# Two-block transformer on one core: the compressed keys' norm ahead on VectorE, the low-rank keys' scale two units later, and two unread products on TensorE

## The reference

```python
# half A: 8 query heads over 2 key heads, head width 64, three branches
kc = apply_rope(rmsnorm(compress(k_cmp), kc_gain))     # 15 compressed keys per key head: 30 rows of 64
p_c = masked_softmax(q @ kc, cmp_end <= t)             # branch 1: compressed
# branches 2 and 3: selected blocks and a window, which for 256 positions are all causal keys
out_a = g0 * (p_c @ vc) + g1 * (p_s @ v_slc) + g2 * (p_w @ v_win)
# half B: 8 low-rank heads, width 96 (64 without and 32 with a rotation)
q, k = rmsnorm(q, q_gain), rmsnorm(k, k_gain)
q, k = rope of the last 32 columns of each
out_b = softmax(q @ k * 96 ** -0.5, causal) @ v
mixed = concat(rmsnorm(out_a), rmsnorm(out_b)) @ w_out
h = x + mixed
return h + peer_ffn(rmsnorm(h))                        # 16 experts for each of 8 heads and position, gathered from HBM
```

## Time and profile before

| | before |
|---|---|
| median of 3 runs | 1548.1 us (1545.95 to 1549.3) |
| the profiled execution's own time | 1549.46 us |
| its span, first to last instruction | 1547.7 us |
| PE busy | 1345.1 us, 87% |
| DVE busy | 966.0 us, 62% |
| ACT busy | 554.8 us, 36% |
| POOL busy | 361.1 us, 23% |
| mean granted clock of PE | 0.935 of full |
| DMA | 407.37 MB, 263 GB/s over the span |

### The profile page before, as it was taken

How to read it: one execution, slowest core, us unless ns; L and a number is a source line. 1 busy time by engine, 2 the same in 40 slices (tenths; PEclk the granted TensorE clock), 3 DMA queues, 4 the chain that set the end, 5 groups by cost and what they waited for, 6 DMA issues and landing times.

```text
span 1547.7 us, 19406 instructions
## 1 busy us (share of the span) xinstructions
PE 1345.1 (87%) x6346; PEld 951.5 (61%) x6346; DVE 966.0 (62%) x2292; ACT 554.8 (36%) x1147; POOL 361.1 (23%) x364
## 2 busy tenths in 40 slices
PE   6997899997997999979798587989798878888877
PEld 4896789986986998968487443434343434343333
DVE  3485655555456555565786667677767777677753
ACT  3453544444554444453573222222212222222221
POOL 0102000000001000010510444444444444345440
PEclk9997999998998999989899899989999999899988
DMA  9524456554313755544401599999999999999995
GB/s 345 216 82 90 143 190 190 190 185 168 109 55 113 230 187 190 163 152 146 170 1 55 199 420 421 420 421 421 421 422 421 422 421 421 422 421 422 421 420 224
DMA packets 97323, 407.37 MB, mean 263 GB/s; under 512 B 6875, under 2 KB 44444, under 8 KB 60412
## 3 DMA queue, kind: packets, MB, share of 16 engines
q0 software_dynamic: 39632, 277.12, 43.8%
q1 hardware_dynamic: 57644, 129.66, 24.6%
HBM read 405.42 MB, written 1.07 MB: 263 GB/s over the span
## 4 chain that ended last, share of the span: by engine, by line
PE 48%; DMA 24%; issue 12%; DVE 11%; ACT 3%; POOL 2%; DVEq 0%; SPq 0%; POOLq 0%; ACTq 0%
DMA arena_v<-in_peer_uv,prob 17%; PE ps L579 12%; PE ps L580 12%; PE ps L581 12%; PE ps L685 6%; DMA uv_mk<-in_peer_uv,prob 3%; DMA arena_u<-in_peer_uv,prob 2%; DVE w_low L1478 1%; PE ps L517 1%; POOL small L1322 1%; PE ps L659 1%; DMA ring<-in_v_a 1%; PE ps L526 1%; PE ps L510 1%; DVE arena_u L2045 1%
## 5 line engine op out<-in xcount | busy, mean ns | idle before, releaser
L1478 DVE TENSOR_TENSOR w_low<-ring,w_high 128x1024 fp32r<-128x1024 f32 (+1 forms) x168 | 195.3, 1205 | 202.3 <-ACT w_high L966 202.0
L966 ACT ACTIVATE w_high<-ring 128x1024 fp32r<-128x1024 f32 (+1 forms) x168 | 166.1, 1038 | 243.2 <-PE ps L581 243.2
L685 PE MATMUL ps<-arena_u,sco 128*128 128x512 f32 x256 | 132.3, 642 | 55.7 <-ACT sco L1138 55.7
L579 PE MATMUL ps<-hT_high,w_high 128*128 128x256 f32 x512 | 145.1, 283 | 0.3
L580 PE MATMUL ps<-hT_low,w_high 128*128 128x256 f32 x512 | 144.7, 283 | 0.0
L581 PE MATMUL ps<-hT_high,w_low 128*128 128x256 f32 x512 | 144.7, 283 | 0.0
L1138 ACT ACTIVATE sco<-const,prob 128x128 f32<-128x128 f32 x256 | 83.9, 391 | 165.0 <-DVE prob L2055 154.1
L1149 ACT ACTIVATE prob<-prob 128x4 f32<-128x4 f32 (+1 forms) x65 | 13.4, 206 | 346.6 <-DVE prob L2045 346.6
L1328 POOL TENSOR_SCALAR small<-small 128x1 f32<-128x1 f32 x8 | 4.2, 529 | 531.6 <-ACT arena_v L996 531.6
L685 PE MATMUL ps<-arena_v,sco 128*128 128x512 f32 x256 | 125.1, 613 | 0.0
L685 PEld LDWEIGHTS ps<-arena_u,sco 128*128 128x128 f32 x256 | 49.1, 200 | 117.6 <-ACT sco L1138 71.8
(11 more groups left out here) (362 smaller groups left out, 2960.1 us busy)
## 6 DMA issues: line engine op xcount, KB each, us to landing
ring<-in_w_up SPq DMA_DIRECT2D x32, 1024.0 KB, 5.6
ring<-in_w_down SPq DMA_DIRECT2D x32, 1024.0 KB, 4.8
qkring<-in_qk_a SPq DMA_DIRECT2D x8, 1024.0 KB, 5.6
qkring<-in_qk_b SPq DMA_DIRECT2D x8, 1024.0 KB, 4.7
ring<-in_peer_wq SPq DMA_DIRECT2D x8, 1024.0 KB, 9.0
ring<-in_w_in SPq DMA_DIRECT2D x8, 860.0 KB, 4.5
ring<-in_v_a SPq DMA_DIRECT2D x4, 1024.0 KB, 12.8
ring<-in_w_out_a SPq DMA_DIRECT2D x4, 1024.0 KB, 9.4
```

What stands on the lines that cost most here:

```text
L579: pe.matmul(dst, a[0], b[0], start=start, stop=False, skip_group_check=True)
L685: last = pe.matmul(ps[2 * t + n][:, :], diag[:, k % N_DIAG, :], slots[k][:, D + n * HALF:D + (n + 1) * HALF], start=False, stop=(final and ...
L966: sc.activation(w_split[pair][0][:, part], ring[:, slot, part], ACT.Copy)\
L1478: ve.tensor_tensor(w_split[pair][1][:, part], ring[:, slot, part], w_split[pair][0][:, part].bitcast(F32), ALU.subtract)\
```

## The change

Five edits, all inside `hybrid_attention`.

1. On DVE the two calls for `mk` leave their place ahead of the compressed keys: `low_rank_mean(1)` now stands behind `kc_ready`, and `low_rank_weigh(mk, gain_mk)` where `low_rank_scale(1, mk)` stood.
2. `low_rank_scale(1, mk)` moves into step 3 of the loop over units, between `share_of(1, 1)` and `add_bias`.
3. PE turns the low-rank pairs in another order, `LOW_RANK_TURNS` (side 0 is queries, side 1 keys): two query pairs first, then two key pairs. The second wait for `mqk_ready` stands at `n` = 2, which is step 5, instead of `n` = 1.
4. ACT's `take_low_rank` follows the same table.
5. PE issues `N_IDLE` = 2 products of 128x512 into `ps[7]`, behind the transposes of `nat` and ahead of the wait for `kc_ready`. Nobody reads them: `ps[7]` is overwritten by the transposed compressed probabilities.

```diff
--- before.py
+++ after.py
@@ -54,6 +54,7 @@
     [0, 512, 128, 128, 128, 128, 128, 128, 24, 256, 128, 32]).tolist()
 N_CMP = 15
 MLA_HEADS = 8
+LOW_RANK_TURNS = ((0, 0), (0, 1), (1, 0), (1, 1), (0, 2), (1, 2), (0, 3), (1, 3))
 QK = 96
 
 P_HEADS = 8
@@ -62,6 +63,7 @@
 N_UNITS = P_HEADS * NT
 CHOOSE_STEPS = 47
 GROUP = 4
+N_IDLE = 2
 N_DIAG = 4
 PEER_SLOT = 2
 
@@ -847,6 +849,8 @@
                     if c % 2:
                         last.then_inc(sem("turned_a"), 1)
 
+                for _ in range(N_IDLE):
+                    pe.matmul(ps[7][:, :], ident, nat[:, 0, 0:HALF], start=True, stop=True)
                 pe.wait_ge(sem("kc_ready"), count.take("kc_ready"))
                 pe.transpose(ps[5][:, P:P + 30], kc_twice, ident[0:30, 0:30]).then_inc(sem("kc_turned"), 1)
                 pe.wait_ge(sem("hT_a"), count.take("hT_a", 4))
@@ -873,12 +877,13 @@
 
                 def turn_low_rank(n, bank):
 
-                    if n < 2:
+                    if n in (0, 2):
                         pe.wait_ge(sem("mqk_ready"), count.take("mqk_ready"))
+                    side, pair = LOW_RANK_TURNS[n]
                     for head in range(2):
                         for t in range(NT):
                             last = pe.transpose(ps[bank][0:QK, head * S + t * P:head * S + t * P + P],
-                                                (mq, mk)[n % 2][:, t, 2 * (n // 2) + head, :], ident)
+                                                (mq, mk)[side][:, t, 2 * pair + head, :], ident)
                     last.then_inc(sem("m_turned_a"), 1)
 
                 pe.wait_ge(sem("c_out"), count.take("c_out", 2))
@@ -1247,7 +1252,8 @@
                 def take_low_rank(n, bank):
 
                     sc.wait_ge(sem("m_turned_a"), count.take("m_turned_a"))
-                    sc.activation((mqT, mkT)[n % 2][:, 2 * (n // 2):2 * (n // 2) + 2, :],
+                    side, pair = LOW_RANK_TURNS[n]
+                    sc.activation((mqT, mkT)[side][:, 2 * pair:2 * pair + 2, :],
                                   ps[bank][0:QK, :].rearrange("p (h s) -> p h s", h=2), ACT.Copy).then_inc(sem("mT_a"), 1)
 
                 sc.wait_ge(sem("c_sco_ready"), count.take("c_sco_ready"))
@@ -1818,8 +1824,6 @@
 
                 low_rank_mean(0)
                 low_rank_weigh(mq, gain_mq)
-                low_rank_mean(1)
-                low_rank_weigh(mk, gain_mk)
 
                 ve.wait_ge(sem("kcv_done"), count.take("kcv_done"))
                 then(ve.tensor_copy(kcv, ps[5][0:30, 0:P]))
@@ -1835,6 +1839,7 @@
                      spread(cos[0:30, 48:56], (0, 1), (0, 1), (1, 8)), spread(sin[0:30, 48:56], (0, 1), (0, 1), (1, 8)),
                      (1, 1, 8))
                 ve.tensor_copy(kc_twice[:, HD:P], kc).then_inc(sem("kc_ready"), 1)
+                low_rank_mean(1)
                 low_rank_scale(0, mq)
 
                 ve.wait_ge(sem("pool_cleared"), count.take("pool_cleared", 3))
@@ -1857,7 +1862,7 @@
                 ve.wait_ge(sem("gates_ready"), count.take("gates_ready"))
                 then(ve.tensor_tensor(spread(c_share, (8, 2), (1, 8)), spread(c_share, (8, 2), (1, 8)),
                                       spread(gates, (24, 2), (3, 8)), ALU.mult))
-                low_rank_scale(1, mk)
+                low_rank_weigh(mk, gain_mk)
                 for t in range(NT):
                     ve.wait_ge(sem("c_weighed"), count.take("c_weighed"))
                     ve.tensor_tensor(nat[:, t, 0:HALF].rearrange("p (h d) -> p h d", d=HD),
@@ -1908,6 +1913,8 @@
                 for u in range(2, 14):
                     take_probT(u % 2)
                     share_of(u - 2, u % 2)
+                    if u == 3:
+                        low_rank_scale(1, mk)
                     if u == 12:
                         out_rms(0)
                     if u == 13:
```

## The result

The changed kernel takes **1555.6 us** (median of 5 runs, 1553.43 to 1556.05) against 1548.1 of the kernel before (5 runs, the three of above among them, 1545.17 to 1553.5): ratio 1.0045, 95% interval 1.0026 to 1.0064. It is slower by some 7 us. The forecast was 1548.4, with 1550.9 at the top of the range, so it was wrong. All ratios compare fast runs alone, and one slow run of the kernel before, at 3362.0 us, is in none of them.

What follows compares the result with a forecast made beforehand. The prediction took mostly PE and DMA to bound the kernel, and PE the units of the attention stage. Its terms, −2.6 + 1.4 + 1.5 = +0.3 us, gave 1548.4 against the median 1548.1; range 1545.4 to 1550.9, 8 in 10.

Steps and rivals of the forecast that it cites:

- The compressed keys, earlier: Ahead of the compressed scores: DVE copies `kcv` at 760.5 instead of 763.11; `kc` reaches PE at 763.9, bounds 763.6 and 764.4.
- The two unread products: The filler, ahead of PE's wait for `kc`: 1.8 us at full clock, costing at most 0.3; half clock 1.8 more.
- The clock, first effect: At the compressed scores: the idle stretch before the fall at 767.7 goes; softmax starts 2.6 us earlier, bounds 2.9 and 2.1.
- the prediction's own sign of being wrong: Ahead of the units: a clock fall at 767 in spite of the two unread products would show the prediction wrong.
- The key scale in unit 3: DVE's inserted 1.76 us delays the probT copy, so PE stalls 1.4 us in unit 4; bounds 1.0 and 1.76.
- The clock, second effect: Behind the compressed scores: PE idles, the clock falls from 770 to 774, slowing the weighed sum; +1.5 us, 0.6 to 2.5.
- The third rival: The second low stretch lasts into the units: +1.8 us, 1549.9; over 0.2% slower only if some 9.5 us long. Chance 0.13.

Runs made afterwards that it cites:

- e2: The change plus seven unread 128x256 products in PE's three waits behind the compressed scores; 1548.1 us, ratio 0.9999 to the kernel before.
- e4: The change with the key scale directly behind the key gain, not in unit 3; 1550.6 us, ratio 1.0019 to the kernel before.
- e9: The change plus seven unread products in PE's waits behind the scores, key scale on POOL; 1547.3 us, ratio 0.9987 to the kernel before.
- e11: The change with the key scale on POOL instead of DVE; 1551.7 us, ratio 1.0022 to the kernel before.
- e13: The change plus two more unread products in each of units 2 to 4; 1554.0 us, ratio 1.0026 to the kernel before.
- e14: The changed kernel, unaltered, measured a third time; 1552.0 us, ratio 1.0023 to the kernel before.
- e10: The change plus seven unread products in the waits behind the scores, without the two ahead of kc_ready; 1549.8 us, ratio 1.0007.
- e12: The change with seven unread products behind the scores, key scale on POOL, without the two ahead of kc_ready; 1547.8 us, ratio 0.9999.
- e1: The change without the two unread products; 1550.7 us, ratio 1.0014 to the kernel before.
- e5: The changed kernel, unaltered, measured again; 1554.4 us, ratio 1.0034 to the kernel before.
- e6: The kernel before with only the new turning order and the key scale in unit 3; 1550.2 us, ratio 1.0018.
- e3: The kernel before plus only the two unread products ahead of the wait for kc_ready; 1551.5 us, ratio 1.0023.
- e7: The change without the two unread products, key scale directly behind the key gain; 1550.7 us, ratio 1.0012 to the kernel before.
- e8: The kernel before plus seven unread products in PE's three waits behind the compressed scores; 1549.8 us, ratio 1.0015.

## Why the prediction was wrong

- **The compressed keys, earlier: right, with one size off.** DVE's copy of `kcv` was forecast for 760.5; PE's product came 1.14 later in this execution (760.96 against 759.82 in the earlier trace rows), and the copy 1.2 later, at 761.70. POOL's 16-column power took 4.35 again, not 3.8: it ended 0.5 us behind the square sum. So the term was at its late bound, and `kc` was there at 765.25. What was wrong is the 3.8: the prediction spread the 1.45 us lost over all of the 2.4 beside DVE's products. In all 16 profiles this power takes 4.35 when a DVE product of 1536 columns is running as it begins, 28 times, and 2.9 when none is, 4 times, even though one begins beside it later (766.10 in the trace before, during the power from 764.50). By these rows what counts is the product in progress at its start, with 1.6 us to go; the prediction's other figure, 4.5 by a full stop for those 1.6, was the nearer.
- **The two unread products: the reading of the clock failed.** I took 1.8 us at full clock and put the half clock aside, because the clock was 1.00 there in the earlier trace rows. In the profiled execution it fell at 762.29, under the turning of `nat`; the filler took 2.58, and `kc` was turned 1.57 us after it was ready (766.82 − 765.25). The prediction had priced that case at 1.8, and gave it no chance. In e2, e4, e9, e11, e13 and e14 the filler ran in 1.88 at full clock.
- **The clock, first effect: the number right where the filler ran at full clock, the reason in part.** In e2 and e14 the softmax starts 2.47 earlier; forecast −2.6. But the fall was not taken away: in e2, e4, e9, e11 and e14 it comes 30.2 to 30.3 us from the first turning, which is 767.7 to 767.8 in the time of the trace before. That is the prediction's own sign of being wrong ("if the clock falls at 767 in spite of the filler"). The scores were through by then, since they began 1.8 earlier (27.77 us from the first turning in e2 and e14, 29.58 before), and that is why they ran in 1.97. The filler has a part in it: without it the fall comes at 26.9 in e10 and e12, ahead of the scores, and at 30.3 in e2 and e9. In the profiled execution the softmax came −1.41, for the filler's sake.
- **The key scale in unit 3: right in mechanism, a little high.** The forecast was +1.4; e1, e2, e5, e6 and e10 show 1.23 or 1.24. The last releaser was ACT's copy of the turned pair, which the prediction named beside probT, and not probT, which it wanted to see in the profile. Under the low clock the term vanishes, as PE is then the slower (DVE waits 1.42 and 1.45 for it in units 2 and 3 of the change).
- **The clock, second effect: the step that failed.** That the clock would fall again where PE stands behind the scores was right: PE was busy 1.64 of 3.94 us, and the clock fell at 775.94. Less the 0.89 of later start that is 775.0, a microsecond behind the forecast's "somewhere from 770 to 774"; in e4, e11 and e14 it fell at 767.7 to 767.8 by the same count, two ahead of it. The size was wrong. The term was +1.5 with bounds of 0.6 and 2.5; it measured 0.87 on the weighed sum (2.86 against 1.99) and, with the stall of unit 4 hidden in it, 6.46 in the units: 7.3 for term and stall together, where the sum had 2.9. In e4, e11 and e14 the weighed sum took 3.78, 1.79 over. The error is one assumption, that a low stretch lasts the 6.8 us of the one example in the earlier trace rows. It lasted 17.1 and 23.9. The third rival had the right mechanism and even its point of decision ("only if the stretch lasts some 9.5 us"), but its chance rested on that one length. The profile of before holds four longer ones outside the rows that I read, at 122.6 for 17.1 us, at 354.7 for 10.2, and these two (the columns again):

```profile
685.80:699.50 13.70, 7.63 (x25) 6.06 (x26) 11.36 (x12) 7.25 (x12) 3.71 (x9) 0.50 0.26 89
877.00:894.10 17.10, 3.14 (x4) 1.51 (x5) 14.12 (x55) 1.48 (x5) 13.67 (x12) 0.50 1.00 414
```

PE is busy 7.63 of 13.70 and 3.14 of 17.10 us in them, and 9.70 of 17.07 in the first. They don't tell that the clock stays low under a full PE, but they forbid to take 6.8 as the length. The one at 354.7 gave a hint of the other too: from 355.7 to its end PE was busy 8.31 of 9.22 us, and the clock stayed low.
- **What was settled**: the slow units are the clock and not the scale, the turning or the rope (e4, e11; e5 against e14), and products in the waits keep the stretch short behind the filler (e2, e9). The two unread products cost time by themselves (e3). **What is open**: why the clock stays low through units in which PE is never idle, why one execution of the same program has the stretch and another not, and whether e7's longer executions have it without the filler. PE's busy time ahead doesn't tell them apart: 6.33 of 10.10 us in e5, where it held, and 6.48 of 10.24 in the change, where it fell (4.84 and 1.64 above).

## What to carry to other kernels

A change that empties PE for a few us is not priced by the wait alone: read in the whole profile how long low stretches of the granted clock last, the longest too, and price the units behind at half rate with a chance of its own. Profile the same program more than once where the clock matters, since one execution here had a stage of 86.14 us and another 91.57. Price unread products by what they did here: seven in three waits won 4 to 7 us over the change (e2), and nothing that the intervals show where the clock had fallen ahead of them (e8; e10 with 1.0007 beside e1 with 1.0014); two in one wait cost 3.6 us on the kernel before (e3).

## What the runs showed of the hardware

- A low stretch can go on under full use: in the change the granted clock stood at 0.50 from 779.35 to 793.01, 13.7 us in which PE was busy in every moment with turnings and products of 64 to 256 columns in fp32, and went to 1.00 in the midst of the same kind of work. The Trainium skill ("TensorE: Matmul & The Clock Gate", "Part 1: The HAM clock gate") says that activity releases the throttle; where activity is taken to mean a busy PE, these rows don't bear it out, and no run here says which work would have counted. The same part says that how many matmuls run slowly differs from run to run; by that the traces agree, with 86.14 and 91.57 us for the stage of one program.
- DVE and POOL slow each other from both sides, and it matters which of them began first. POOL's power of 16 columns took 4.35 us when it began beside a running DVE product of 1536 columns and 2.9 when such a product began beside it (28 and 4 cases); the product that began second took 1.74, no longer than others. The key gain on DVE took 2.17 us instead of 1.75 where a step of POOL's rope was running as it began; the rope's last step, begun beside the gain, took 2.24 instead of 0.72 (775.05 and 791.41 in the change). A four-column DVE product took 1.10 instead of 0.17 beside a POOL product of 1536 columns, and ended with it (e9).
